# A recurrence on one core: where the half products of a modulation group stand

## The reference, cut to what matters

```python
def step(S, inp):
    r_t, w_t, k_t, v_t, kk_t, a_t = inp
    sa = jnp.einsum('bhvk,bhk->bhv', S, -kk_t)
    S = (S * w_t[:, :, None, :] + sa[..., None] * (kk_t * a_t)[:, :, None, :]
         + v_t[..., None] * k_t[:, :, None, :])
    y = jnp.einsum('bhvk,bhk->bhv', S, r_t) if emit else None
    return S, y
```

```python
sh1, sc1, g1, sh2, sc2, g2 = [m[:, None, :] for m in
    jnp.split(jax.nn.silu(c) @ w_ada[l] + b_ada[l], 6, axis=-1)]
```

## Time and profile before

| | us |
|---|---|
| median of 3 runs | 3979.51 |
| lowest and highest run | 3977.25, 3980.0 |
| the profiled execution | 3977.37 |
| its span | 3975.7 |
| TensorE busy in it | 3779.7 (95%) |
| VectorE busy | 2505.8 (63%) |
| ScalarE busy | 1731.2 (44%) |
| GpSimd busy | 272.9 (7%) |

### The profile page before, as it was taken

How to read it: one execution, slowest core, us unless ns; L and a number is a source line. 1 busy time by engine, 2 the same in 40 slices (tenths; PEclk the granted TensorE clock), 3 DMA queues, 4 the chain that set the end, 5 groups by cost and what they waited for, 6 DMA issues and landing times.

```text
span 3975.7 us, 86377 instructions
## 1 busy us (share of the span) xinstructions
PE 3779.7 (95%) x36054; PEld 3216.3 (81%) x36054; DVE 2505.8 (63%) x4455; ACT 1731.2 (44%) x3155; POOL 272.9 (7%) x437
## 2 busy tenths in 40 slices
PE   6999999889889999999999999999999999899999
PEld 2788888566666799989999999977778778787879
DVE  2544588655655687687888888764552553646465
ACT  3544333434433445446454454552343442535354
POOL 0000011222223100000000000000000000000000
PEclk8999999899989999999999999999999999999999
DMA  9422566555656587565776767532222232433335
GB/s 374 151 79 61 189 228 193 175 173 177 183 174 180 189 284 231 193 231 165 224 230 217 229 214 224 192 133 85 76 68 90 71 123 93 136 117 97 117 105 191
DMA packets 289441, 662.41 MB, mean 167 GB/s; under 512 B 21089, under 2 KB 31329, under 8 KB 287537
## 3 DMA queue, kind: packets, MB, share of 16 engines
q1 hardware_dynamic: 233392, 441.73, 34.3%
q0 software_dynamic: 55680, 215.34, 17.3%
HBM read 639.16 MB, written 17.83 MB: 165 GB/s over the span
## 4 chain that ended last, share of the span: by engine, by line
PE 82%; DVE 9%; ACT 3%; DMA 3%; issue 3%; SPq 0%; POOL 0%; DVEq 0%; ACTq 0%; POOLq 0%
PE psum L854 65%; PE psum L820 2%; PE psum L1116 2%; DMA ada_head<-in_w_ada 1%; PE psum L1166 1%; DVE wlo L2217 1%; PE psum L879 1%; DVE smx L2987 1%; ACT whi L1574 1%; PE psum L1181 1%; PE psum L1047 1%; PE psum L957 1%; PE psum L941 1%; PE psum L942 1%; PE psum L1111 1%
## 5 line engine op out<-in xcount | busy, mean ns | idle before, releaser
L2217 DVE TENSOR_TENSOR wlo<-raw,whi 128x512 fp32r<-128x512 f32 (+3 forms) x1568 | 1047.3, 680 | 944.1 <-ACT whi L1574 933.7
L1574 ACT ACTIVATE whi<-raw 128x512 fp32r<-128x512 f32 (+3 forms) x1568 | 971.2, 623 | 1425.3 <-PE psum L854 1398.9
L854 PE MATMUL psum<-hhi,whi 128*128 128x512 f32 (+1 forms) x2416 | 831.3, 344 | 35.9 <-DVE hlo L2260 17.6
L854 PE MATMUL psum<-hhi,wlo 128*128 128x512 f32 (+1 forms) x2416 | 811.4, 336 | 0.0
L854 PE MATMUL psum<-hlo,whi 128*128 128x512 f32 (+1 forms) x2416 | 811.3, 336 | 0.0
L854 PEld LDWEIGHTS psum<-hhi,whi 128*128 128x128 f32 x2416 | 460.8, 191 | 132.7 <-issue 56.1
L854 PEld LDWEIGHTS psum<-hlo,whi 128*128 128x128 f32 x2416 | 461.3, 191 | 46.1 <-issue 2.2
L854 PEld LDWEIGHTS psum<-hhi,wlo 128*128 128x128 f32 x2416 | 460.4, 191 | 47.1
L854 PE MATMUL psum<-fhi,whi 128*128 128x256 f32 x1408 | 400.9, 285 | 6.9 <-issue 4.5
L854 PE MATMUL psum<-flo,whi 128*128 128x256 f32 x1408 | 400.5, 284 | 0.0
L854 PE MATMUL psum<-fhi,wlo 128*128 128x256 f32 x1408 | 400.5, 284 | 0.0
(11 more groups left out here) (441 smaller groups left out, 6944.4 us busy)
## 6 DMA issues: line engine op xcount, KB each, us to landing
raw<-in_w_in SPq DMA_DIRECT2D x328, 512.0 KB, 3.9
ada_raw<-in_w_ada POOLq DMA_DIRECT2D x192, 512.0 KB, 4.7
red_raw<-in_w_adaT POOLq DMA_DIRECT2D x128, 512.0 KB, 4.7
raw<-in_w_out SPq DMA_DIRECT2D x96, 512.0 KB, 3.7
raw<-in_w_gate SPq DMA_DIRECT2D x88, 512.0 KB, 4.9
raw<-in_w_val SPq DMA_DIRECT2D x88, 512.0 KB, 4.3
raw<-in_w_down SPq DMA_DIRECT2D x88, 512.0 KB, 4.9
ada_head<-in_w_ada SPq DMA_DIRECT2D x64, 512.0 KB, 10.4
```

The source lines that it names most:

```text
L854: mm = pe.matmul(dst, l, r, start=(k == 0 and i == 0 and first), stop=(k == nch - 1 and i == 2), skip_group_check=True)
L1574: act.activation(whi[:, lc % HL, 0:width], raw[:, (lc // 2) % RAW, lc % 2, 0:width], ACT.Copy).then_inc(w_hi, 1)
L2217: dve.tensor_tensor(wlo[:, lc % HL, 0:width], raw[:, (lc // 2) % RAW, lc % 2, 0:width], whi[:, lc % HL, 0:width].bitcast(F32), ALU.subtrac ...
```

## The change

In each trip the third group of the modulation (j = 2) gives up three places: half 3 behind GH0, half 4 behind Q, half 5 behind GH1. Its last five half products, 3 to 7, stand one each in steps 1 to 5 of the scan. Before, the scan had two, half 6 in step 1 and half 7 in step 3. The order among half products and the number of instructions are the same.

```diff
--- before.py
+++ after.py
@@ -1303,15 +1303,12 @@
                 dve_at("W0")
                 act_at("WU0")
                 chunk_steps(0)
-                ada(2, 3)
                 dve_at("W1")
                 act_at("WU1")
                 chunk_outputs(0)
                 done(chunk_outputs(1), "Q")
-                ada(2, 4)
                 dve_at("GH0")
                 chunk_steps(1)
-                ada(2, 5)
                 for i in range(1, 7):
                     for d in range(2):
                         dve_at(f"GH{d}" if i == 1 else f"Z{d}{i - 1}")
@@ -1320,8 +1317,8 @@
                         done(mm, f"Z{d}{i}")
                     if i == 1:
                         chunk_pairs(done, 0)
-                    if i in (1, 3):
-                        ada(2, 5 + (i + 1) // 2)
+                    if i < 6:
+                        ada(2, 2 + i)
                     if i == 6:
                         ada_final(it * 3 + ADA_HEAD + 2)
                 dve_at("Z16")
```

## The result

The changed kernel takes 3993.89 us, the median of seven runs (3989.06 to 3999.52), against 3980.0 for the one before, also in seven (3977.25 to 3987.3). The ratio is 1.0031 with a 95% interval of 1.0021 to 1.0042, so it is slower by 8.4 to 16.7 us. The profiled execution took 3996.07 us.

A forecast was written before the change was run, and what follows sets the result against it. The prediction put 82% of the span on TensorE, with VectorE setting the pace up to `hd` and in the scan. Buffer wait +15.6 and stalls -5.6 gave +10.0 us on 3979.5: 3989.5 us, range 3978 to 4005.

The forecast's parts named there:

- a wait for a buffer: In the scan, halves 6 and 7 reuse buffers of halves 3 and 4: 1.6 to 2.3 us a trip, +15.6 us.
- What is removed: Three half products leave their places before the scan, 0.57 us each at full clock; no gain, since `hd` doesn't move.
- The engine time in the steps: Half products in scan steps 2 to 5: 0 at full clock, 0.27 us a step at the low one.
- The wait ahead of half 6: In scan step 4 TensorE waits 2.3 us for its load at full clock; the next update comes 1.6 us late.
- The wait ahead of half 7: In scan step 5: none at full clock; at the low one the load lands just as it is wanted.
- The stalls: TensorE's issue stalls in the recurrence, 13.7 us in eight trips, move partly into the scan and hide there: -5.6 us.
- Rival 1: The wait comes in full and the clock falls with it in the recurrence: 3998 to 4010 us, chance 0.17.
- rivals 2 and 3: Wait paid back by clock or stalls, 3975 to 3984 us, chance 0.20; both at once, 3965 us, chance 0.08.

The follow-up runs named there:

- second pair: A second profile each of the kernel before and the changed kernel, both unedited; ratios to the kernel before 1.0001 and 1.003.
- e6: Changed kernel, but half 3 stays behind GH0 and halves 4 to 7 stand in steps 1 to 4; ratio 1.0011 to the kernel before, 3988.92 us.
- e7: Changed kernel with half of the bytes (256 KB) in the third group's loads of halves 6 and 7, sums incomplete; ratio 0.9984 to the kernel before, 3975.76 us.
- e2: Changed kernel with four buffers for the halves in place of three; ratio 0.9996 to the kernel before, 3981.32 us.
- e8: Changed kernel with halves 3 to 5 in steps 1 to 3, half 6 in step 5, half 7 and transposes behind the state outputs; ratio 1.0014, 3989.48 us.
- e4: Changed kernel with one of the four products in the third group's halves 3 to 6, sum incomplete; ratio 1.0012 to the kernel before, 3987.73 us.
- before_again: The kernel before, unedited, measured against itself and profiled a second time; ratio 1.0001.
- e3: The kernel before with four buffers for the halves in place of three, order unchanged; ratio 0.9991 to the kernel before, 3980.14 us.
- e5: Changed kernel with 32 columns in place of 256 in the third group's halves 3 to 6, sum incomplete; ratio 1.0012 to the kernel before, 3988.73 us.

## Why the prediction was right, and where it was not

The forecast was 3989.5 with 3978 to 4005, and slower as the likeliest. The time is 3993.9. The mechanism was the one forecast: a wait for a buffer in the scan. One term was far too small: the scan lost 26.2 us where 15.6 were forecast. The total came within 4 us in part by luck, since 4.5 us were gained in stretches for which I had forecast nothing.

**What is removed: right.** The three half products gave nothing back. Trip 5 in the chain after, the answer to the earlier trace rows:

```profile
1109.39 0.70 DVE hd L2628
...
1110.14 0.37 PE psum L1316 x2
...
1110.62 1.71 PE psum L1062 x62
1112.32 1.05 PE psum L820 x8
```

The pair behind `hd` starts when `hd` ends, as before; the joined products then run through in 1.71 us. TensorE's groups by line (busy us, mean ns, then idle before), against the earlier trace rows:

```profile
L1188 PE MATMUL psum<-b_tok,wu 64*64 64x64 f32 x512 | 20.9, 228 | 13.0 <-DVE hd L2628 11.8 <-issue 1.1
...
L1062 PE MATMUL psum<-b_s,a_s 64*64 64x64 f32 x480 | 19.4, 246 | 0.0
```

GH1's first product waits for `hd` 11.8 us in all, where it waited 2.3 us. The 16 half products removed ahead of it are 16 x 0.57 = 9.1 us of work, and it became 9.5 us of waiting. Still, the way from the solve to `hd` is 3.6 us shorter (1.2 in the second pair), where I had expected no change; the half products don't explain it.

**The engine time in the steps: right in its unit, rare in fact.** I had 0.27 us a step at the low clock. The one trip that shows it (trip 6) has steps of 1.60 and 1.40 us between updates 2 and 4. The clock was full there in most trips, so it came to 0.3 us in all.

**The wait ahead of half 6: right.** I had 1.6 us for a trip at full clock and 2.06 at the low one. Updates 4 to 5 are longer by 14.7 us in eight trips (13.2 in the second pair), 1.6 to 1.8 a trip on average, 0.9 to 3.3 in single ones.

**The wait ahead of half 7: mis-sized.** I wrote that half 7 "is no longer waited for" at full clock and just in time at the low one, which is 0 to 0.3 us a trip. It is 11.5 us (11.0), 1.4 a trip. The failed step is the 4.3 us for its load. That was the median of loads a step and more apart; here halves 6, 7 and the next trip's half 0 are issued about 1 us apart, and half 7's takes 4.6 to 6.4 us. e6 shows that it is the place behind another load, with 4.0 to 4.2 us as the first, and e7 that it is the bytes: with half of them in both loads 3.0 to 3.6. The kernel before had told as much. Its page of the profile gives a median of 4.7 us for these loads:

```profile
ada_raw<-in_w_ada POOLq DMA_DIRECT2D x192, 512.0 KB, 4.7
```

And its own load of half 7, issued 0.9 to 2.5 us behind the one ahead of it in trips 2 to 7, took 5.0 to 6.3 us there, but 4.1 and 4.2 in trips 1 and 8, over 3 us behind.

The load isn't the whole of it. An estimate, with each trip's own issue times and product times and 4.3 us for the load: 4.7 of the 11.5 us would be left (4.0 of 11.0). They come mostly from the low clock, at which half 7 takes 1.01 us in place of 0.57 in seven of eight trips (six), where I had half of them, and from GpSimd's issue in trip 1, 1.90 us behind the end of half 4.

**The stalls: gone from the joined products, but not into the scan.** I took -5.6 us for "four tenths" of 13.7, which is 5.5. The joined products indeed gained 6.4 (8.1) us and show no stall in the rows above. But between them and update 6 TensorE has no issue stall either, in both profiles; from update 6 to the next solve it has 18.0 us of them where the kernel before has 15.4 (18.8 and 14.6). The sum of stalls in the trips fell by 5.6 in one pair of profiles and by 0.4 in the other. A shift of the stall points is not a saving. That some are hidden in the time in which TensorE waits for the load, as I had forecast, is not shown. Nor is their cause: the profile names nothing that TensorE waits for in them.

**The rivals.** The time at the low clock did not grow with the wait: 75.1 us in the recurrence before and 75.1 after (81.9 and 61.4 in the second pair). Rival 1 holds in one place only, at half 7, as above: in e2, without the wait ahead of half 6, half 7 takes 0.57 us in all eight trips. In e2 and e7, where the waits are short, the low clock takes 41.0 us, but 75.1 in e8, whose scan is as short; so what brings the clock back, as rivals 2 and 3 need it, isn't shown. It is worth little: from update 6 through the first key products takes 3.47 us at full clock instead of 4.34, under 1 us a trip, not the 2 that I had priced. e7 alone came out faster than the kernel before.

**The sum.** 15.6 - 5.6 = 10.0 forecast; in the first pair +26.2 in the scan, -6.4 in the joined products, and -4.5 in all the rest, 15.3; in the second +24.2, -8.1 and -1.8, 14.3.

What stays open: why the stretch from update 6 to the next solve differs by up to 11 us between kernels that are the same there (371.7 in e4, 382.4 in e7), with one profile each, and with it where e2's gain in the joined products went in each trip.

## What to carry to other kernels

Moving work into idle slots moves the uses of its buffers together: count, for each buffer, the time from one use to the next that needs it reloaded, and compare it with the whole round (release, issue, landing), here 5 us for 512 KB. When a load is issued while another is still under way, price it with the other's bytes as well; look up what such loads took in the trace, not only those that stood alone. Work that ends before something the engine waits for anyway is free where it stands; taking it away gains nothing.

## What was not expected of the hardware

- Four products of 128x32 with 128x256, placed in four column groups of the array, cost no more than one of them: 0.57 us to the next product at full clock in both cases (e4 against the earlier trace rows). Fewer columns do shorten it: 0.20 us with 32.
- A load of 512 KB by GpSimd's queue lands in 4.1 us alone, one of 256 KB in 3.1; a second of 512 KB issued 0.95 us behind takes 5.5; the same load issued as the first (e6) takes 4.0 to 4.2.
- Issue stalls moved with the order of the code: in three profiled kernels with three half products more ahead of the joined products (before, before_again, e3) they take 19.3 to 20.6 us from `hd` to their end, in seven without them (the changed kernel twice, e2, e4, e5, e7, e8) 12.2 to 16.0.
